# Local attentions by pairs of heads, with their roots and forget sums moved to earlier stages

## The reference, cut to what matters

```python
def fox_mixer(z, f_bias, q_gain, k_gain):
    q, k, v, f = jnp.split(z, [FOX_WIDTH, 2 * FOX_WIDTH, 3 * FOX_WIDTH], axis=-1)
    q = rms_norm(split_heads(q, FOX_HEADS), q_gain)
    k = rms_norm(split_heads(k, FOX_HEADS), k_gain)
    log_f = jax.nn.log_sigmoid(f.astype(jnp.float32) + f_bias).transpose(0, 2, 1)
    return merge_heads(forgetting_attention(q, k, split_heads(v, FOX_HEADS), log_f))
# forgetting_attention: c = cumsum(log_f); s = q k^T * scale + c_q - c_k; causal softmax; p v
# moba_mixer: rope(rms_norm(q)), rope(rms_norm(k)); causal softmax attention within the one block
```

## Time and profile before

| | us |
|---|---|
| time, median of 3 runs | 2408.41 (2407.76 to 2408.49) |
| the profiled execution | 2396.61 |
| its span in the trace | 2394.8 |
| TensorE busy | 2197.3 (92%) |
| VectorE, ScalarE, GpSimd busy | 1003.1, 1159.0, 1205.6 |
| mean granted TensorE clock | 0.961 of full |

### The profile page before, as it was taken

The page is one execution under the profiler, slowest core; times in us unless marked ns, Lnnn a source line. Parts: engine busy times, 40 slices in busy tenths (PEclk is TensorE's granted clock), DMA queues, the critical chain, the costliest instruction groups (busy, mean ns, idle before and its releaser), DMA issues. The chain is left out here.

```text
span 2394.8 us, 41799 instructions
## 1 busy us (share of the span) xinstructions
PE 2197.3 (92%) x17910; PEld 1977.9 (83%) x17910; DVE 1003.1 (42%) x2016; ACT 1159.0 (48%) x1663; POOL 1205.6 (50%) x308
## 2 busy tenths in 40 slices
PE   8999989899999999889899999888978777998998
PEld 7999865489999999865488999766857777998998
DVE  2332754424222222565334221376656777333551
ACT  5544532466345434632356443555874554554443
POOL 6776610075878877630074876432310000675785
PEclk9999999899999999999999999898998988999999
DMA  7555422253556555431243655321213111553553
GB/s 258 169 170 171 154 72 89 70 176 123 194 171 200 185 176 180 141 123 64 97 141 111 199 180 172 114 70 53 72 58 103 37 34 40 192 170 127 176 179 115
DMA packets 304102, 319.02 MB, mean 133 GB/s; under 512 B 7897, under 2 KB 295117, under 8 KB 303405
## 3 DMA queue, kind: packets, MB, share of 16 engines
q1 hardware_dynamic: 303917, 316.34, 41.3%
HBM read 313.10 MB, written 3.21 MB: 132 GB/s over the span
## 5 line engine op out<-in xcount | busy, mean ns | idle before, releaser
L558 POOL TENSOR_TENSOR slab_lo<-ring,slab_hi 128x2048 fp32r<-128x2048 f32 (+2 forms) x188 | 843.5, 4499 | 560.0 <-ACT slab_hi L549 560.0
L549 ACT CAST slab_hi<-ring 128x2048 fp32r<-128x2048 f32 (+2 forms) x188 | 347.6, 1851 | 412.6 <-PE bank L449 284.9
L444 PE MATMUL bank<-x_parts_hi,slab_hi 128*128 128x256 f32 x1760 | 436.4, 286 | 0.5 <-ACT slab_hi L549 0.5
L445 PE MATMUL bank<-x_parts_lo,slab_hi 128*128 128x256 f32 x1760 | 431.6, 283 | 0.0
L444 PEld LDWEIGHTS bank<-x_parts_hi,slab_hi 128*128 128x128 f32 x1760 | 337.4, 192 | 3.8 <-issue 2.6
L445 PEld LDWEIGHTS bank<-x_parts_lo,slab_hi 128*128 128x128 f32 x1760 | 337.5, 192 | 1.2 <-issue 1.0
L379 POOL TENSOR_TENSOR slab_lo<-ring,slab_hi 128x2048 fp32r<-128x2048 f32 (+1 forms) x54 | 243.7, 4538 | 127.4 <-ACT slab_hi L368 91.9
L449 PE MATMUL bank<-x_parts_hi,slab_lo 128*128 128x256 f32 x1760 | 247.8, 283 | 7.8 <-POOL slab_lo L558 7.8
L449 PEld LDWEIGHTS bank<-x_parts_hi,slab_lo 128*128 128x128 f32 x1760 | 226.9, 192 | 9.4 <-POOL slab_lo L558 9.4
L411 PE MATMUL bank<-hidden_hi,slab_hi 128*128 128x256 f32 x704 | 194.4, 276 | 0.0
L412 PE MATMUL bank<-hidden_lo,slab_hi 128*128 128x256 f32 x704 | 194.3, 276 | 0.0
(11 more groups left out here) (659 smaller groups left out, 4972.2 us busy)
## 6 DMA issues: line engine op xcount, KB each, us to landing
ring<-in_ffn_w_in SPq DMA_DIRECT2D x88, 1024.0 KB, 5.1
ring<-in_ffn_w_out SPq DMA_DIRECT2D x32, 1024.0 KB, 5.1
ring<-in_w_in SPq DMA_DIRECT2D x27, 1024.0 KB, 5.3
ring<-in_mix_w_in SPq DMA_DIRECT2D x24, 1024.0 KB, 5.3
ring<-in_w_mod SPq DMA_DIRECT2D x24, 1024.0 KB, 5.1
ring<-in_w_up SPq DMA_DIRECT2D x22, 1024.0 KB, 5.1
ring<-in_ffn_w_out SPq DMA_DIRECT2D x16, 768.0 KB, 4.4
ring<-in_mix_w_out SPq DMA_DIRECT2D x8, 1024.0 KB, 5.2
```

The lines of the kernel that those rows point to most:

```text
L444: pe.matmul(out, w[0][:, k, col], act[0][:, k, :], start=(k == 0), stop=False)
L445: pe.matmul(out, w[0][:, k, col], act[1][:, k, :], start=False, stop=False)
L549: act.copy(self.hi[p][:, 0:w], K.ring[n % RING][:, 0:w]).then_inc(self.hi_ready, 1)
L558: pool.tensor_tensor(self.lo[p][:, 0:w], place[:, 0:w], self.hi[p][:, 0:w].bitcast(F32), ALU.subtract)\
```

## The change

1. The units become eight pairs of heads, 2m and 2m+1, which share a query tile (`PairAttention`). In a pair the two heads' products are issued in turn: the scores of one read features 0 to 63 and go to bank 0, those of the other read features 64 to 127 and go to bank 1; the outputs go to rows 0 to 63 and 64 to 127 of one bank. One ScalarE copy takes out both heads' transposes, and one both outputs. The maximum, the exponential and the scaling stay one operation per head. There are ten steps in place of eighteen.
2. Each step holds two scan steps and eight modulation products (4, 2 and 2), so that all nine slabs are used up in steps 0 to 8.
3. The squares, head sums, Ln and Exp of q and k move into the inverse block (`LocalRoots`): squares first on ScalarE, sums on TensorE after all masks are read, Ln and Exp on ScalarE after the diagonals and before the substitution's result. Modulation slab 0 moves ahead of the sums, as soon as unit 8 has been masked, and slabs 1 and 2 stand behind them; TensorE enters the rest of the inverse only when the Ln are done.
4. The forget sums move into the projections (`ForgetSums`): the bound before `heads(11)`, one small Exp on ScalarE ahead of `evacuate(12)`, and the polynomial and running sum between `heads(11)` and `heads(12)`.
5. In the attention block the order on VectorE is: gains, eight scalings, the scan's state, then the steps, with the two rotations inside step 0. On TensorE: scan 0, both rotations, scan 1, then the steps; a wait for the rotations stands in step 0 after four modulation products.

```diff
@@ project_stage, ScalarE
+                act.wait_ge(forget_in, 1)
+                act.activation(forget.e, forget.e, ACT.Exp).then_inc(forget_exp, 1)
                 evacuate(12)
@@ project_stage, VectorE
+                own.after(dve, last)
+                forget.dve_bounded(dve, s["f"], col("f_bias")).then_inc(forget_in, 1)
                 heads(11)
+                dve.wait_ge(forget_exp, 1)
+                forget.dve_sums(dve)
                 heads(12)
@@ new: LocalRoots
+    def pe(self, pe):
+        for i in range(4):
+            pe.wait_ge(self.squared, i + 1)
+            pe.matmul(self.K.bank[self.BANK + i][:, :], self.K.c("headsum"),
+                      self.sq[:, 2 * i:2 * i + 2, :].rearrange("p a t -> p (a t)"), start=True, stop=True)\
+                .then_inc(self.summed, 1)
@@ rwkv_stage, TensorE
+                    pe.wait_ge(intra_read, 9)
+                    mod.pe_first(pe, 0, 1)
                     pe.wait_ge(intra_read, 16)
-                    mod.pe_first(pe)
+                    roots.pe(pe)
+                    mod.pe_first(pe, 1, mod.FIRST)
+                    roots.pe_free(pe)
                     inv.pe(pe)
@@ rwkv_stage, ScalarE
-                    inv.act(act, between=lambda i: mod.act_first(act) if i == 1 else None)
+                    roots.act_squares(act)
+                    for g in range(4):
+                        inv.diagonal(act, g)
+                    roots.act_roots(act)
+                    inv.act(act, between=lambda i: mod.act_first(act) if i == 1 else None, first=4)
@@ new: PairAttention
+        for u, bank in zip((a, b), self.SCORES):
+            last = pe.matmul(K.bank[bank][:, 0:n], u["q"], u["k"], start=True, stop=not biased, skip_group_check=True)
+        for j in range(len(a["bias"])):
+            for u, bank in zip((a, b), self.SCORES):
+                last = pe.matmul(K.bank[bank][:, 0:n], *u["bias"][j], start=False, stop=(j == len(a["bias"]) - 1),
+                                 skip_group_check=True)
...
+        for c in range(parts):
+            for u in range(2):
+                last = pe.matmul(K.bank[self.OUT][pair[u]["rows"], 0:P], pair[u]["v"][c],
+                                 self.turned[p % 2][:, u, c * P:(c + 1) * P],
+                                 start=(c == 0), stop=(c == parts - 1), skip_group_check=True)
@@ attention_stage, TensorE
                 scan.pe(pe, 0)
-                for i in range(4):
-                    pe.wait_ge(squared, i + 1)
-                    pe.matmul(K.bank[i][:, :], K.c("headsum"), sq[:, 2 * i:2 * i + 2, :].rearrange("p a t -> p (a t)"),
-                              start=True, stop=True).then_inc(summed, 1)
-                scan.pe(pe, 1)
-                for _ in range(mod.AHEAD):
-                    mod.some(pe)
+                pe.wait_ge(normed, 8)
                 for i in range(2):
-                    pe.wait_ge(normed, 8)
...
-                    scan.pe(pe, 2 + i)
-                pe.wait_ge(fsum_ready, 1)
-                pe.wait_ge(roped, 2)
-                att.pe(pe, between=lambda: mod.some(pe), mid_step=lambda i: scan.pe(pe, i + EARLY))
+                scan.pe(pe, 1)
+                for i in range(len(pairs) + 2):
+                    att.pe_scores(pe, i)
+                    mod.some(pe, 4)
+                    if i == 0:
+                        pe.wait_ge(roped, 2)
+                    scan.pe(pe, EARLY + 2 * i)
+                    att.pe_turn(pe, i - 1)
+                    mod.some(pe, 2)
+                    att.pe_out(pe, i - 2)
+                    scan.pe(pe, EARLY + 2 * i + 1)
+                    mod.some(pe, 2)
                 mod.pe_end(pe)
@@ attention_stage, ScalarE
+                for i in range(len(pairs) + 2):
+                    mod.act_copies(act, i)
+                    scan.act(act, EARLY + 2 * i - 1)
+                    att.act_exp(act, i)
+                    att.act_turned(act, i - 1)
+                    att.act_out(act, i - 2)
+                    scan.act(act, EARLY + 2 * i)
@@ attention_stage, VectorE
+                scan.dve(dve, 0)
+                for i in range(len(pairs) + 1):
+                    att.dve_normed(dve, i - 1)
+                    if i == 0:
+                        rope(0)
+                    scan.dve(dve, EARLY + 2 * i - 1)
+                    att.dve_top(dve, i)
+                    if i == 0:
+                        rope(1)
+                    scan.dve(dve, EARLY + 2 * i)
```

More of the change, by code:

```diff
@@ L1887, in rwkv_stage @@
         mod = Modulations(K, ctx)
+        roots = LocalRoots(K, ctx)
         with ExitStack() as ictx:
@@ L1932, in _ @@
                     inv.pool(pool)
-        attention_stage(K, lt, xt, unit, mod)
+        attention_stage(K, lt, xt, unit, mod, roots.sq)
 class RwkvScan:
@@ L2128, in first_place, with pe_first @@
         return self.K.bank[n % 2][0:2, HALF * (n // 2):HALF * (n // 2 + 1)]
-    def pe_first(self, pe):
+    def pe_first(self, pe, first, end):
         K = self.K
-        for n in range(self.FIRST):
+        for n in range(first, end):
             w = view(K.next_slab(pe))
@@ L2146, in act_first, with some @@
         self.copies = self.FIRST
-    def some(self, pe):
+    def some(self, pe, count):
         K = self.K
-        for _ in range(self.AT_A_CALL):
+        for _ in range(count):
             if self.n == MOD_SLABS:
@@ L2161, in some, with act_copies @@
                 self.k, self.n = 0, self.n + 1
-    def act(self, act, step, calls):
+    def act_copies(self, act, upto):
         K = self.K
-        while self.copies < min(MOD_SLABS, self.FIRST + (self.AHEAD + step * calls) * self.AT_A_CALL // KD):
-            n = self.copies
+        for n in range(self.copies, min(MOD_SLABS, self.FIRST + upto)):
             K.wait_slabs(act, self.n0 + n + 1)
@@ L2174, in pe_end @@
         K = self.K
-        while self.n < MOD_SLABS:
-            self.some(pe)
+        self.some(pe, KD * MOD_SLABS)
         pe.wait_ge(self.copied, MOD_SLABS)
@@ L2340, in attention_stage @@
         normed, rotated, roped = K.sem("qk_normed"), K.sem("qk_rotated"), K.sem("qk_roped")
-        fabs_ready, fexp_ready, fsum_ready = K.sem("f_abs"), K.sem("f_exp"), K.sem("f_sum")
-        units = []
+        pairs = []
         for kind in range(2):
-            for h in range(4):
-                rows = slice(64 * (h % 2), 64 * (h % 2) + 64)
+            for m in range(2):
                 for i in range(TT):
[L2347 to L2354, removed]
-                        one = K.c("ident", slice(0, 4), first=h, n=1)
-                        u["bias"] = [(fc[:, i * P:(i + 1) * P], one.to_broadcast([4, n])),
-                                     (one.to_broadcast([4, P]), fneg[:, 0:n])]
-                    units.append(u)
@@ L2359, in attention_stage @@
-        att = Attention(K, ctx, "mix_at", units, ((0, 1), (2,), (3,)), T)
+                    pair = []
+                    for h in (2 * m, 2 * m + 1):
+                        rows, n = slice(64 * (h % 2), 64 * (h % 2) + 64), P * (i + 1)
+                        one = K.c("ident", slice(0, 4), first=h, n=1)
+                        pair.append({"keys": n, "rows": rows,
+                                     "q": qk[rows, 4 * kind + m, i * P:(i + 1) * P],
+                                     "k": qk[rows, 4 * kind + 2 + m, 0:n],
+                                     "mask": K.c("causal")[:, P - i * P:2 * P],
+                                     "v": [v[:, c, 256 * kind + 64 * h:256 * kind + 64 * h + 64] for c in range(i + 1)],
+                                     "bias": [(forget.sums[:, i * P:(i + 1) * P], one.to_broadcast([4, n])),
+                                              (one.to_broadcast([4, P]), forget.minus[:, 0:n])] if kind == 0 else [],
+                                     "out": y[:, 6 * kind + m, i * P:(i + 1) * P]})
@@ L2426, in _, with rope @@
                 sin = K.sin[:, :].unsqueeze(1).to_broadcast([P, 2, T])
-                scan.dve(dve, 2)
-                for i in range(2):
+                def rope(i):
                     t = slice(4 + 2 * i, 6 + 2 * i)
@@ L2436, in _ @@
                     dve.tensor_tensor(qk[:, t, :], qk[:, t, :], rot[:, :, :], ALU.add).then_inc(roped, 1)
-                att.dve(dve, at_step=lambda i: scan.dve(dve, i + EARLY - 1), normed_first=True)
+                scan.dve(dve, 0)
[8 more added lines that the diff above has]
+                    scan.dve(dve, EARLY + 2 * i)
+                for step in range(EARLY + 2 * len(pairs) + 1, scan.GATE + 4):
+                    scan.dve(dve, step)
                 mod.dve(dve)
```

168 lines of the change are left out of this document (134 added, 34 removed).

## The result

The changed kernel takes 2380.02 us (median of 4 runs, 2377.72 to 2381.83) against 2408.09 for the kernel before on the same chip: a ratio of 0.9898, interval 0.9871 to 0.9925, or 28 us less by the medians (25 by the ratio). Forecast were 36 less, 2372, with a range of 2361 to 2385. The profiled execution took 2381.83, its span 2379.9. Sign, range and most terms held; one term was off by a factor of nine, and it hides a kernel that is 30 to 34 us faster still.

The account below looks back on a forecast made before the run. TensorE's queue and what it waits for were taken to bound the attention block; per layer -9.3 - 3.65 - 6.6 + 1.5 = -18.1 us, -36.1 in all, taking 2408.4 to 2372.3 us, range 2361 to 2385.

Parts of the forecast that it names:

- rival E: Next stage's start: the gain is given back waiting for the ring's three slabs, no change, 2408 us; chance 0.03.
- Term 1: Attention block: pairing heads shortens TensorE's scores, transposes and outputs from 27.7 to 18.4 us, -9.3 us per layer.
- Rival C: Paired attention products: the two halves don't run together, saving only 4.7 us there, 2381 us; chance 0.06.
- Term 2: Head sums leave the attention queue, -3.65 us per layer, at no cost in the inverse block (bounds 0 and +3).
- Rival D: Inverse block becomes late by its new roots, +3 us per layer, 2378 us; chance 0.05.
- Term 3: Forget sums moved into the projections cost 0 there (bounds 0 and +2), with at most a 1.2 us GpSimd hold.
- Rival F: Projections: GpSimd's slab holds each two-input operation of the forget sums 3 us, slower by 27, 2435 us; chance 0.04.
- Term 4: Attention block: waits and slow clock fall from 14.4 to 7.8 us, -6.6 per layer (bounds -10 and +2).
- Rival B: Attention block: waits don't shrink, term 4 is 0, -11.5 us per layer, 2385 us; chance 0.17.
- Term 5: Clock dips after new TensorE idles at the attention start and before `inv_x`: +1.5 us per layer, bounds 0 and +5.

Follow-up runs that it names:

- e3: Changed kernel with the two heads of a pair issued one after the other, in scores and outputs; 2387.26 us, ratio 0.9913 to before.
- e1: Changed kernel with the scan's state zeroed before gains and scalings instead of behind them; 2359.32 us, ratio 0.9805 to before.
- e5: e1 plus one idle TensorE product of 512 columns in each of step 0's two waits (rotation, state); 2346.12 us, ratio 0.9774 to before.
- e8: Kernel before with only roots and forget sums moved, no pairs, and the scan's state zeroed behind the eight scalings; 2407.48 us, ratio 1.0013 to before.
- e2: Changed kernel, order untouched, with three idle TensorE products of 512 columns in the 3.0 us wait at the start; 2363.98 us, ratio 0.9834 to before.
- e6: e1 with the second rotation behind the scan's first state update, its wait in step 1, step 0's slab products as 4 and 4; 2346.70 us.
- e7: Changed kernel with e6's late rotation and slab products as 4 and 4, state still zeroed behind the scalings; 2367.18 us, ratio 0.9846 to before.
- e9: e6 with one idle 512-column product ahead of the slab products in steps 1 and 3; 2349.68 us, ratio 0.9771 to before.
- e10: e6 with the first scan step of each step placed between the scores and the four slab products; 2349.16 us, ratio 0.9769 to before.

## Why the prediction came out as it did

**The bottleneck, held.** TensorE's queue and its waits set the block's end in every kernel of the study, and nothing at the next stage's start gave the gain back (rival E): the blocks gained 14.6 us, the profiled execution 14.8.

**Term 1, products of the attentions (-9.3), held.** Forecast for pairs: scores 1.48 and 2.54, transposes 0.61, outputs 0.42 and 0.69. Measured: 1.51 and 2.56, 0.53, 0.37 and 0.71. Rival C is out by e3 and by the outputs' 0.71.

**Term 2, head sums (-3.65), held.** 3.65 us left the queue and took 3.70 in the inverse block, whose length did not change. The slack at `sol_solved` was 1.6 us, where at least 1.1 was promised. Rival D is out.

**Term 3, forget sums (0), held with less to spare.** `heads(12)` ended at 313.73, forecast at 312.3: the hold by GpSimd's slab was 3.3 us and not 1.2, since it began at the first operation behind the Exp, with one tensor input, and not at the first with two. Rival F stayed out; it was one hold and no more.

**Term 4, waits, held in kind.** Forecast against measured: start 3.1 and 3.0, the wait for the second rotation 1.4 and 1.2, state 1.05 and 0.2, square 1.5 and 1.3, root 0.5 and 0.5, the rest 0.2 and 0. In sum 7.8 and 6.2. The state's 0.2 is no merit of the order: the four slab products ahead of it ran at the low clock (1.87 us, 374.71 on the timeline), and in e1 this wait is 1.0. The clock at the block's end is 1.00 as foretold. Rival B, that the waits don't shrink, is out too. Its total (2385) lies nearer to the measured time than the forecast, as those of C (2381) and D (2378) do.

**Term 5, clock dips elsewhere (+1.5, bounds 0 and +5), failed.** This is the wrong step of the sum. From 117.7 take the 14.4 of waits and slow clock, 9.3 and 3.65; add the 6.2 of waits: 96.6 us at full clock. The block took 110.4, so the slow clock cost 13.8 us per layer, nine times the value and almost three times the upper bound. The sum closes: -9.3 - 3.65 - 8.2 + 13.8 = -7.3. It also closes in the other direction: e5, at full clock, keeps 2.0 us of waits (1.3, 0.5 and 0.2) and has 2.2 of idle products in place of the two others; 90.4 of work (96.6 less 6.2) and these make 94.6, and it took 92.6. By e5's work the slow clock's cost would be 15.8, so it lies between 14 and 16 us.

The mistake was in how the row was read and what it was applied to. The prediction took 5 us at 0.51 behind the idle of the earlier trace rows, supposed that 2 to 3 us of TensorE's work would meet such a stretch, and entered 1.5. In that trace the clock is low from 324.1 to 330.9, 1.7 us of it still in the idle, and the loss was covered: the next product waited another 1.07 us for VectorE (339.89). Here the queue behind the wait had no cover. TensorE ran at 1.2 GHz for 10.2 us (357.1 to 367.3); the clock fell again 6.8 us after it had returned, 1.7 us behind the end of the 1.2 us wait for the rotation, and stayed low for 20.5 us. e8 shows the first part by itself: 19 us in all, or 9.5 per layer, from a wait of 3.0 that was summed at 3.1; in its trace the wait and half of the 10.2 us make 8.1. e1 gets back 10 to 11 per layer from the same wait, e5 another 4 to 7 (by ratios, by medians) from the two small ones and what follows them. The prediction did say that a granted clock of 0.5 after the first waits would show it wrong, and priced that at 5 us at most.

The Trainium skill, "TensorE: Matmul & The Clock Gate", section "HAM oscillation — how this bites in real kernels", warns that idle gaps between bursts of products bring the clock down to half. The trace agrees in kind for the first fall, behind 3.0 us. The fall in e7 is not of this kind: from 357 until it came, near 381, TensorE had idled for 0.14 us.

**The total, in part luck.** The forecast started from the profiled execution, 2396.6, and came to 2360.5 for it; the changed kernel's profiled execution took 2381.8. That is a miss of 21 us, and a gain of 14.8 where 36 were forecast. The median misses by 8 only because the prediction also carried over the 11.8 us by which the kernel before's median lay above its trace, and the changed kernel's median has no such distance. No run shows where those microseconds were; they made up for 13 of the 21.

**What stays open.** Shown is that the first slow stretch comes from the first wait (e1, e2, e8: taken away, filled, put in). What starts the later ones is not settled. Filling the two waits of step 0 removed them in e5's profiled execution; reordering the same waits away (e6, e7) did not remove them altogether, nor did a filler or an order nearer to the place (e9, e10). e5's two idle products may act through the waits that they fill or by being there. e5 and e6 are equal in time, 2346.12 and 2346.70, within their spreads. The best kernels of the study are these two, 2.3% faster than before and 1.2 to 1.4% faster than the change as made.

## What to carry to other kernels

When an in-order TensorE queue begins a stage, the operation that releases it goes first on the other engine, however short: one memset of 0.48 us behind 3.5 us of scalings cost 19 to 22 us over two layers. Price an idle of TensorE by what the clock does to the work queued behind it, over the whole slow stretch (10.2 us here), and ask whether that work is covered; a price read where it was covered is too low. When a large restructuring yields less than its sum, look at the granted clock in windows of 5 us before you doubt the sum: here every product group was within 0.1 us of its forecast and every wait but one within 0.2. And compare like with like: a trace stands for one execution, and a forecast built on it should be held against a trace first.

## What the runs showed of the hardware that was not expected

- A VectorE operation with one tensor input and a constant (L2499, 4x256, fp32) ended 0.15 us behind GpSimd's slab, 3.54 us long instead of 0.28; in layer 2 it is the same, 3.52 and 0.15. So not only operations with two tensor inputs are held, as the prediction had read the earlier trace rows. The Trainium skill, "SBUF — State Buffer", section "Who interferes with whom", says that `tensor_scalar` too can take the port pair that VectorE and GpSimd share; the trace agrees by these two rows.
- Three idle products of 512 columns in a 3 us wait (e2) made the kernel 15 us faster than leaving TensorE idle.
- The slow stretch behind the 3.0 us wait was 10.2 us long in both layers of after and in e7 and e8.
- A slow stretch can begin when TensorE has been busy for over 20 us but for 0.14 (e7, near 381), in products of 4 rows or 2 columns; the same products ran at 1.00 in e5's trace.
- Executions of one kernel differ by more than usual where slow stretches remain: e7 has 2356.47 to 2376.16, e2 2359.01 to 2376.6.
